# The last expert pair's down weights by halves of the output columns, and the second mixer's first chunk by token blocks, in a model block on one core

## The chip, the cores and the metric

The kernel runs on one core of a Trainium2 chip. The metric is the device time of one execution in microseconds (us), from the first to the last instruction of the core; less is better. TensorE (PE) multiplies, VectorE (DVE), ScalarE (ACT) and GpSimd (POOL) work on elements, SyncE (SP) issues most of the weight loads.

## The reference

256 tokens of width 1024 pass through two blocks. Only this much of the first matters here; the second block (four feed-forward layers and two recurrent mixers) follows it.

```python
for i in range(DEPTH):                       # DEPTH = 2
    mix = even_or_odd_mixer(x, ...)          # i = 1: _mla_gla_mixer, which begins with x @ w_in
    x = _layer_norm(ALPHA * x + mix, ln1_g[i], ln1_b[i])
    ffn = _hier_moe(x, ...)                  # 32 experts, 2 of them for each token
    x = _layer_norm(ALPHA * x + ffn, ln2_g[i], ln2_b[i])

# one expert, with d = 1024 and a hidden width of 512
hdn = jax.nn.silu(xb @ w_gate[e]) * (xb @ w_up[e])
y = hdn @ w_down[e]
```

## The kernel before

Each engine runs a program written out by hand, and semaphores order them against each other. The programs have three parts: part 0 ends in the middle of layer 0's experts, part 1 goes from there to the middle of layer 1's experts, and part 2 does the rest. So the end of an expert stage occurs twice: in part 1 ahead of the second mixer (`od_pe`, `od_act`, `od_dve`), and in part 2 ahead of the first feed-forward layer (`ffn_pe`).

The 32 experts are worked in 16 pairs. The two experts j = 0 and 1 of a pair hold 64 tokens each; the products of expert 0 go to the PSUM partitions 0 to 63, those of expert 1 to 64 to 127, so one product uses 64 of the array's 128 columns (the trace writes 128*64). The weights are float32 and are multiplied as such; the trace records one float32 product as two MATMULs. `paired_pe` (line 1345) takes the products of the two experts in turn. Each pair has 12 loads of 1 MB: gate, up and down, in two halves of the contraction each, for each expert. They go through one queue in the order of use, into a ring of 7 slots and into further places that are lent to it for the stage (`w_parts`, `arena`, `x_high_slot`, `x_low_slot`, `x_tok`).

For pair g PE does gate, up, the combining products of pair g - 1 for token block 0 (`combine_pe`), the transposes of the hidden values, the combining products of block 1, and down into two banks of 512 output columns, n = 0 and 1. The result y is cut into a high and a low part: ACT writes `yh` (line 1438), DVE writes `yl` (line 1468). `combine_pe` multiplies both by the selection matrix (line 228, 128x512), and DVE adds the product to `acc` (`add_dve`, line 1377). `combine_pe` runs for token blocks tb = 0, 1 and for the column halves n = 0, 1 of each.

After the last pair, DVE adds, takes the layer norm's statistics by half rows (`half_stats`, line 665), then mean and variance (672, 674), centres (676), and scales (687) with the reciprocal root that POOL makes. PE transposes the normed tokens (`transpose_x_pe`, line 479), ahead of them go idle products that write nothing of use (`busy_pe`, line 460, 128x512 with the full 128 columns). ACT takes the high part of the transposed tokens (line 495), DVE the low part (504, `x_low_dve`). The weights of the mixers and feed-forward layers are likewise cut in high (432, ACT, `split_act`) and low (439, DVE, `split_dve`) parts, in buffers of half a 1 MB chunk; `ahead` is the first such part of the next stage. `project_pe` multiplies tokens and weights by three products for each pair of parts; a chunk of the second mixer is named `od(i)`, its two parts `od(i) + (0,)` and `od(i) + (1,)`. `project_block_pe` does one token block of a chunk and waits for the low part of its second half.

Of the kernel before, what the change touches and what calls it, by code (L numbers as in the profile page):

```python
# [465 lines left out]

def transpose_x_pe(e, k, n, after=None):
    S = k.S
    for tb in range(NB):
        if n < 0:  # L470
            e.wait_ge(*S.x_loaded[tb][0])
        for half in range(2):
            view = pairs(k.banks.open(e, B_BANKS, ("xT", n, tb, half))[:, :], 4)
            if n >= 0 and half == 0:
                busy_pe(e, k, k.banks["xT", n, tb, half], BUSY[after][tb])
            if n >= 0:
                e.wait_ge(*S.x_tok[n, tb, half])
            for i in range(4):
                ins = e.transpose(view[:, i, :], k.x_tok[:, tb, block(4 * half + i)], k.ident)
            ins.then_inc(*S.turned.tell((n, tb, half)))  # L480
# [187 lines left out]
def norm_centre_dve(e, k, n, tb):  # L668
# [5 lines left out]
    e.tensor_scalar(k.ve[:, tb:tb + 1], k.mv[:, tb, 1:2], LN_EPS, None, ALU.add).then_inc(*S.variance.tell((n, tb)))  # L674
    e.wait_ge(*S.norm_loaded[n])
# [674 lines left out]
def combine_pe(e, k, X, g, tb):  # L1350
# [3 lines left out]
    for n in range(2):  # L1354
# [31 lines left out]
def experts_pe(e, k, X, first, last):  # L1386
    S, b = X.S, k.experts
    gather_pe(e, k, X, first // GATHERED)
    for g in range(first, last):
# [21 lines left out]
        paired_pe(e, k, X, tiles, "down", g, FT_E // 2, b.hT)  # L1411
    for tb in range(NB):
        combine_pe(e, k, X, last - 1, tb)


def experts_act(e, k, X, first, last, ahead=None):
# [3 lines left out]
    for g in range(first, last):  # L1420
# [20 lines left out]
def experts_dve(e, k, X, first, last, ahead=None):  # L1441
# [6 lines left out]
    for g in range(first, last):  # L1448
# [14 lines left out]
        if ahead is not None and g == last - 1:  # L1463
            split_dve(e, k, ahead)
        for n in range(2):
            cols = slice(BANK * n, BANK * n + BANK)
# [1479 lines left out]
```

## Time and profile before

| What | us |
|---|---|
| median of 3 runs | 2320.6 |
| lowest and highest of them | 2320.22, 2322.26 |
| profiled execution, first to last instruction | 2323.1 |
| PE busy | 2166.1 (93%) |
| DVE busy | 1142.2 (49%) |
| ACT busy | 784.0 (34%) |
| end of layer 0's experts to the first projection of the second mixer | 634.70 to 660.38 |
| end of layer 1's experts to the first feed-forward product | 1284.07 to 1308.65 |

The profiled execution has no time of its own beside its span; the span is 2.5 us, or 0.1%, above the median. In a timeline a row gives start, duration, engine, line, operation, what is written from what, shape and count; in brackets stands how long the engine had been idle before it, and who ended that. Several instructions can be merged in one row. Matmul records have about 0.16 us at their end in which the next one already runs.

### The profile page before, as it was taken

To read this page: it belongs to the slowest core of one execution; us is meant where nothing else is said; L and a number is where in the kernel's file an instruction comes from. 1 tells how busy PE (TensorE), PEld (TensorE's weight loads), DVE (VectorE), ACT (ScalarE), POOL (GpSimd) and SP (SyncE) were. 2 spreads that over 40 slices of the span, in tenths; PEclk is the share of its full clock that TensorE was granted. 3 is DMA by queue.
4 is the path that set the end of the run, shared out by engine and by line. 5 is a ranking of instruction groups with operands and counts; after the bars stand their busy time and mean duration, and the time that the engine had idled before them with its cause. 6 is when DMAs were issued, how large, how long until landed. Compare 5 with 4: busy or idle time off the path is not lost.

```text
span 2323.1 us, 30109 instructions
## 1 busy us (share of the span) xinstructions
PE 2166.1 (93%) x12126; PEld 1528.0 (66%) x12126; DVE 1142.2 (49%) x1786; ACT 784.0 (34%) x1299; POOL 61.5 (3%) x62
## 2 busy tenths in 40 slices
PE   8999998899887989997988999999999999989998
PEld 7884443443367944433433688898888788888887
DVE  5582222121156831211111666678666766787666
ACT  3441110111034321101111355454555455554553
POOL 0010000000010100000000000001000000001000
PEclk9999999899998799999999999999999999999999
DMA  9449999999972289999999864634555464534561
GB/s 289 145 175 379 421 421 421 417 421 420 413 246 73 76 363 420 420 421 415 420 420 421 295 209 168 199 128 127 181 200 200 154 208 166 193 96 159 167 208 46
DMA packets 231542, 622.66 MB, mean 268 GB/s; under 512 B 15456, under 2 KB 166944, under 8 KB 182112
## 3 DMA queue, kind: packets, MB, share of 16 engines
q1 hardware_dynamic: 226096, 605.32, 68.7%
q0 software_dynamic: 3040, 10.78, 1.5%
q10 hardware_dynamic: 2256, 4.50, 0.5%
q8 instruction: 102, 1.67, 0.3%
q14 instruction: 48, 0.39, 0.0%
HBM read 619.51 MB, written 1.05 MB: 267 GB/s over the span
## 4 chain that ended last, share of the span: by engine, by line
PE 41%; DMA 6%; DVE 4%; ACT 2%; issue 1%; POOL 0%; SPq 0%; DVEq 0%; ACTq 0%
PE bank L1517 14%; PE bank L1505 10%; PE bank L1518 7%; PE bank L228 6%; PE bank L1345 3%; DMA arena<-in_moe_w_up 1%; DMA ring<-in_moe_w_up 1%; DMA ring<-in_ffn_gate 1%; DMA w_parts<-in_moe_w_up 1%; DMA x_tok<-in_moe_w_up 1%; DVE w_low L439 1%; PE bank L1673 1%; ACT w_high L432 1%; DVE x_tok L687 0%; DVE x_tok L676 0%
## 5 line engine op out<-in xcount | busy, mean ns | idle before, releaser
L439 DVE TENSOR_TENSOR w_low<-ring,w_high 128x1024 fp32r<-128x1024 f32 x364 | 441.1, 1225 | 271.7 <-ACT w_high L432 271.7
L1517 PE MATMUL bank<-xT_parts,w_high 128*128 128x512 f32 x1408 | 496.2, 395 | 6.0 <-DVE xT_parts L504 6.0
L432 ACT ACTIVATE w_high<-ring 128x1024 fp32r<-128x1024 f32 x364 | 377.1, 1053 | 218.0 <-PE bank L1518 184.6
L1518 PE MATMUL bank<-xT_parts,w_low 128*128 128x256 f32 x1408 | 394.5, 280 | 0.0
L1345 PE MATMUL bank<-ring,arena 128*64 128x512 f32 x1344 | 339.0, 594 | 17.3 <-DMA w_parts<-in_moe_w_gate 5.3
L1517 PEld LDWEIGHTS bank<-xT_parts,w_high 128*128 128x128 f32 x1408 | 264.0, 188 | 69.0 <-DVE xT_parts L504 6.9
L1345 PE MATMUL bank<-w_parts,arena 128*64 128x512 f32 x768 | 263.8, 609 | 13.4 <-DMA w_parts<-in_moe_w_up 6.7
L1518 PEld LDWEIGHTS bank<-xT_parts,w_low 128*128 128x128 f32 x1408 | 265.8, 189 | 3.1
L1345 PEld LDWEIGHTS bank<-ring,arena 128*64 128x64 f32 x1344 | 110.1, 137 | 230.5 <-issue 221.9
L1453 DVE SCALAR_TENSOR_TENSOR arena<-arena,bank 128x512 f32<-128x512 f32 x32 | 23.9, 747 | 434.1 <-PE bank L1345 434.1
L228 PE MATMUL bank<-w_high,xT_parts 128*128 128x256 f32 x1152 | 222.9, 290 | 10.4 <-DVE w_low L439 8.8
L228 PEld LDWEIGHTS bank<-w_high,xT_parts 128*128 128x128 f32 x1152 | 186.4, 195 | 13.0 <-ACT arena L564 4.5
L228 PE MATMUL bank<-w_low,xT_parts 128*128 128x256 f32 x576 | 165.0, 286 | 0.0
L1345 PEld LDWEIGHTS bank<-w_parts,arena 128*64 128x64 f32 x768 | 81.1, 140 | 121.3 <-issue 117.0
L1468 DVE TENSOR_TENSOR arena_rounded<-bank,arena_rounded 128x512 fp32r<-128x512 f32 x64 | 41.2, 686 | 217.8 <-ACT arena_rounded L1438 217.8
L1505 PE MATMUL bank<-w_high,hidden_low 128*128 128x512 f32 x320 | 126.3, 395 | 0.0
L1505 PE MATMUL bank<-w_low,hidden_high 128*128 128x512 f32 x320 | 126.2, 394 | 0.0
L1505 PE MATMUL bank<-w_high,hidden_high 128*128 128x512 f32 x320 | 126.1, 394 | 0.0
L228 PE MATMUL bank<-xT_parts,w_high 128*128 128x256 f32 x608 | 115.7, 292 | 9.0 <-DVE xT_parts L504 6.0
L228 PEld LDWEIGHTS bank<-w_low,xT_parts 128*128 128x128 f32 x576 | 112.6, 195 | 0.2
L1438 ACT ACTIVATE arena_rounded<-bank 128x512 fp32r<-128x512 f32 x64 | 34.7, 594 | 229.0 <-PE bank L1345 229.0
L228 PEld LDWEIGHTS bank<-xT_parts,w_high 128*128 128x128 f32 x608 | 98.7, 199 | 10.8 <-issue 5.4
(284 smaller groups left out, 2934.4 us busy)
## 6 DMA issues: line engine op xcount, KB each, us to landing
ring<-in_moe_w_gate SPq DMA_DIRECT2D x56, 1024.0 KB, 24.3
ring<-in_moe_w_up SPq DMA_DIRECT2D x56, 1024.0 KB, 21.0
ring<-in_moe_w_down SPq DMA_DIRECT2D x56, 1024.0 KB, 25.8
ring<-in_ffn_gate SPq DMA_DIRECT2D x44, 1024.0 KB, 6.8
ring<-in_ffn_up SPq DMA_DIRECT2D x44, 1024.0 KB, 5.4
ring<-in_ffn_down SPq DMA_DIRECT2D x44, 1024.0 KB, 6.6
w_parts<-in_moe_w_up SPq DMA_DIRECT2D x32, 1024.0 KB, 26.1
w_parts<-in_moe_w_down SPq DMA_DIRECT2D x32, 1024.0 KB, 26.1
```

The source lines that it names most:

```text
L228: ins = e.matmul(out, lhs, rhs, start=first and i == 0, stop=last and i == len(parts) - 1)
L432: e.activation(hi, src, ACT.Copy).then_inc(*S.high.tell(key))
L439: e.tensor_tensor(lo, src, hi.bitcast(F32), ALU.subtract).then_inc(*S.low.tell(key))
L1345: ins = e.matmul(tile[r, :], lhs[:, half * per + kk, r], X.ring.view(chunks[j])[:, kk, BANK * n:BANK * n + BANK], start=half == 0 and kk = ...
L1438: e.activation(b.yh[:, cols], X.banks[X.key("y", g, n)][:, :], ACT.Copy).then_inc(*S.act_out.tell(X.key("y_high", g, n)))
L1453: e.scalar_tensor_tensor(out=b.silu, in0=b.silu, scalar=b.weight[:, i:i + 1], in1=X.banks[X.key("h", g)][:, :], op0=ALU.mult, op1=ALU.mult ...
L1468: e.tensor_tensor(b.yl[:, cols], X.banks[X.key("y", g, n)][:, :], b.yh[:, cols].bitcast(F32), ALU.subtract).then_inc(*S.dve_out.tell(X.key ...
L1505: ins = e.matmul(out, lhs, rhs[:, 0, cols], start=g == 0 and j == 0, stop=g == FT - 1 and j == 2)
L1517: e.matmul(pairs(bank[:, :]), hi[:, j, :], k.x_parts[:, :, j, :], start=j == 0, stop=False)
L1518: ins = e.matmul(bank[:, 0:T], lo[:, j, :], k.xh[:, j, :], start=False, stop=j == KT - 1)
L1673: ins = e.matmul(scores[:, 2 * i + blk, :], d.decayed[r, j, block(blk)], d.queries(d.decayed[r, j, block(blk)], m), start=True, stop=True)
```

## The change

The four down loads of pair 15 fetch, in place of half of the contraction for all 1024 output columns, the whole contraction for half of the columns (pieces of 512 floats). PE multiplies them with `last_down_pe`: column half 0 for expert 0 and then for expert 1, then the combining products of half 0 for both token blocks, then the same for column half 1. ACT and DVE cut y by column half as each is done. The splitting of `ahead` moves behind that, on DVE behind the second mean. DVE's order of sums, statistics and norm changes with it (`norm_after_experts_dve`), and `norm_centre_dve` is cut in two. In the second mixer, PE transposes token block 0, projects it with `od(0)`, and only then transposes and projects block 1; the idle products ahead of block 1 are gone there. ACT's order of work stays as it is apart from `ahead`.

```diff
+def by_columns(name, g):
+
+    return name == "down" and g == N_PAIRS - 1
+
...
-                    src = rows(w[layer, PAIR * g + j], k)[:, half * per:(half + 1) * per, :]
+                    w_rows = rows(w[layer, PAIR * g + j], k)
+                    src = w_rows[:, :, half * BANK:(half + 1) * BANK] if by_columns(name, g) else w_rows[:, half * per:(half + 1) * per, :]
...
+def last_down_pe(e, k, X, tiles, g, n):
+
+    S, b = X.S, k.experts
+    chunks = [X.key("down", g, n, j) for j in range(PAIR)]
+    for j, chunk in enumerate(chunks):
+        r = slice(CAP * j, CAP * j + CAP)
+        e.wait_ge(*X.ring.landed(chunk))
+        for kk in range(FT_E):
+            ins = e.matmul(tiles[n][r, :], b.hT[:, kk, r], X.ring.view(chunk)[:, kk, :], start=kk == 0, stop=kk == FT_E - 1)
+    ins.then_inc(*S.expert.tell(X.key("down", g, n)))
...
-        paired_pe(e, k, X, tiles, "down", g, FT_E // 2, b.hT)
-    for tb in range(NB):
-        combine_pe(e, k, X, last - 1, tb)
+        if by_columns("down", g):
+            for n in range(2):
+                last_down_pe(e, k, X, tiles, g, n)
+                for tb in range(NB):
+                    combine_pe(e, k, X, g, tb, (n,))
+        else:
+            paired_pe(e, k, X, tiles, "down", g, FT_E // 2, b.hT)
...
-        if ahead is not None and g == last - 1:
-            split_act(e, k, ahead)
-        e.wait_ge(*S.expert[X.key("down", g, 1)])
         for n in range(2):
+            if n == 0 or by_columns("down", g):
+                e.wait_ge(*S.expert[X.key("down", g, n if by_columns("down", g) else 1)])
             cols = slice(BANK * n, BANK * n + BANK)
             e.activation(b.yh[:, cols], X.banks[X.key("y", g, n)][:, :], ACT.Copy).then_inc(*S.act_out.tell(X.key("y_high", g, n)))
...
-    project_pe(e, k, od(0), fresh=n)
+    bank = k.banks.open(e, A_BANKS, od(0))
+    for tb in range(NB):
+        transpose_block_pe(e, k, n, tb, 0 if tb else BUSY["experts"][0])
+        project_block_pe(e, k, od(0), bank, tb, n)
...
-def norm_after_experts_dve(e, k, X, n):
-
+def norm_after_experts_dve(e, k, X, n, ahead):
+
+    g = N_PAIRS - 1
+    y_low_dve(e, k, X, g, 0)
     added_stats_dve(e, k, X, n, 0, 0)
+    added_stats_dve(e, k, X, n, 1, 0)
+    y_low_dve(e, k, X, g, 1)
     added_stats_dve(e, k, X, n, 0, 1)
+    norm_mean_dve(e, k, n, 0)
     norm_centre_dve(e, k, n, 0)
-    added_stats_dve(e, k, X, n, 1, 0)
+    added_stats_dve(e, k, X, n, 1, 1)
     norm_scale_dve(e, k, n, 0)
-    added_stats_dve(e, k, X, n, 1, 1)
+    norm_mean_dve(e, k, n, 1)
+    split_dve(e, k, ahead)
+    x_low_dve(e, k, n, 0, 0)
+    x_low_dve(e, k, n, 0, 1)
     norm_centre_dve(e, k, n, 1)
-    x_low_dve(e, k, n, 0, 0)
     norm_scale_dve(e, k, n, 1)
```

In the order of instructions a matmul counts once for each product, where the trace has two records for a float32 one.

On PE, the second half of the last pair's down products in layer 0 (chunks in `x_low_slot` and `x_tok`), with what follows, stood so before:

```order
L1345 MATMUL bank<-x_low_slot,arena 64x512
L1345 MATMUL bank<-x_tok,arena 64x512
L1345 MATMUL bank<-x_low_slot,arena 64x512
L1345 MATMUL bank<-x_tok,arena 64x512
L228 MATMUL bank<-arena_rounded 128x512 x8
L460 MATMUL bank<-tables 128x512 x4
L479 MATMUL bank<-tables,x_tok 128x128 x8
L460 MATMUL bank<-tables 128x512 x4
L479 MATMUL bank<-tables,x_tok 128x128 x8
```

In the changed kernel all down products of the last pair, with what follows, stand so:

```order
L1374 MATMUL bank<-w_parts,arena 64x512 x4
L1374 MATMUL bank<-x_high_slot,arena 64x512 x4
L228 MATMUL bank<-arena_rounded 128x512 x4
L1374 MATMUL bank<-x_low_slot,arena 64x512 x4
L1374 MATMUL bank<-x_tok,arena 64x512 x4
L228 MATMUL bank<-arena_rounded 128x512 x4
L466 MATMUL bank<-tables 128x512 x4
L484 MATMUL bank<-tables,x_tok 128x128 x8
L228 MATMUL bank<-w_high_53,xT_parts 128x256
```

The products of the two experts no longer take turns: four of one stand ahead of four of the other. The combining products of column half 0 stand ahead of the products of column half 1, and the first projection stands behind the transposes of block 0.

On PE, the second token block of the second mixer's chunk `od(0)` begins so in the changed kernel (`w_high_54` belongs to its second part, and block 0 ends with the first two rows):

```order
L228 MATMUL bank<-w_low_58,xT_parts 128x256
L228 MATMUL bank<-w_high_54,xT_parts 128x256
L484 MATMUL bank<-tables,x_tok 128x128 x8
L228 MATMUL bank<-w_high_53,xT_parts 128x256
L228 MATMUL bank<-w_low_57,xT_parts 128x256
```

The eight transposes of block 1 moved from ahead of the projection to its middle.

On DVE, the end of the norm ahead of the second mixer stood so before, from the last sum on (`w_low_58` is the second part of `od(0)`, `w_low_55` the first of `od(1)`):

```order
L1377 TENSOR_TENSOR acc<-acc,bank 128x512
L665 BN_STATS bn<-acc 128x6
L672 BN_AGGR mv<-bn 128x2
L674 TENSOR_SCALAR var_eps<-mv 128x1
L676 SCALAR_TENSOR_TENSOR x_tok<-acc,mv,norm_gb 128x1024
L504 TENSOR_TENSOR xT_parts<-bank,xT_parts 128x4x128
L687 SCALAR_TENSOR_TENSOR x_tok<-x_tok,rstd,norm_gb 128x512 x2
L504 TENSOR_TENSOR xT_parts<-bank,xT_parts 128x4x128 x3
L439 TENSOR_TENSOR w_low_58<-ring,w_high_54 128x1024
L439 TENSOR_TENSOR w_low_55<-ring,w_high_51 128x1024
```

In the changed kernel it stands so, from the last sum on:

```order
L1405 TENSOR_TENSOR acc<-acc,bank 128x512
L675 BN_STATS bn<-acc 128x6
L703 SCALAR_TENSOR_TENSOR x_tok<-x_tok,rstd,norm_gb 128x512 x2
L682 BN_AGGR mv<-bn 128x2
L684 TENSOR_SCALAR var_eps<-mv 128x1
L445 TENSOR_TENSOR w_low_57<-ring,w_high_53 128x1024
L514 TENSOR_TENSOR xT_parts<-bank,xT_parts 128x4x128 x2
L692 SCALAR_TENSOR_TENSOR x_tok<-acc,mv,norm_gb 128x1024
L703 SCALAR_TENSOR_TENSOR x_tok<-x_tok,rstd,norm_gb 128x512 x2
L445 TENSOR_TENSOR w_low_58<-ring,w_high_54 128x1024
L514 TENSOR_TENSOR xT_parts<-bank,xT_parts 128x4x128 x2
L445 TENSOR_TENSOR w_low_55<-ring,w_high_51 128x1024
```

The splitting of `ahead` (`w_low_57`) and both low parts of block 0 moved between the last mean and the centring of block 1; the splitting of `w_low_58` moved ahead of the low parts of block 1.

## Rows read from the trace of the kernel before

**Rows 1.** The page: the span and the engines' busy times.

```profile
span 2323.1 us, 30109 instructions
PE 2166.1 (93%) x12126; PEld 1528.0 (66%) x12126; DVE 1142.2 (49%) x1786; ACT 784.0 (34%) x1299; POOL 61.5 (3%) x62
```

**Rows 2.** Timeline of PE, end of layer 1's experts.

```profile
1277.81 3.65 PE L1345 MATMUL bank<-arena 128*64 128x512 f32 x16 [1.32 <-DMA arena<-in_moe_w_up]
...
1282.96 1.17 PE L228 MATMUL bank<-arena_rounded 128*128 128x512 f32 x4
1284.07 0.64 PE L1345 MATMUL bank<-w_parts,arena 128*64 128x512 f32 x1
1284.08 0.64 PE L1345 MATMUL bank<-x_high_slot,arena 128*64 128x512 f32 x1
...
1293.77 2.23 PE L228 MATMUL bank<-arena_rounded 128*128 128x512 f32 x8 [2.26 <-DVE arena_rounded L1468]
1295.84 3.60 PE L460 MATMUL bank<-tables 128*128 128x512 f32 x8
...
1308.65 0.47 PE L1517 MATMUL bank<-xT_parts,w_high 128*128 128x512 f32 x1 [1.50 <-DVE xT_parts L504]
```

**Rows 3.** Groups on PE by shape, 686 to 690.5 us: products with 96 and 64 columns.

```profile
L228 PE MATMUL bank<-arena,wide_tables 128*96 128x256 f32 x8 | 1.9, 385 | 0.5 <-DVE arena L2117 0.5
L228 PE MATMUL bank<-arena,wide_tables 128*64 128x256 f32 x4 | 1.1, 392 | 0.0
```

**Rows 4.** Timeline of ACT, end of layer 1's experts.

```profile
1290.64 1.06 ACT L432 ACTIVATE w_high<-ring 128x1024 fp32r<-128x1024 f32 x1 [6.80 <-DMA ring<-in_ffn_gate]
1291.60 1.07 ACT L1438 ACTIVATE arena_rounded<-bank 128x512 fp32r<-128x512 f32 x2
```

**Rows 5.** Timeline of DVE, end of layer 1's experts.

```profile
1292.94 1.28 DVE L1468 TENSOR_TENSOR arena_rounded<-bank,arena_rounded 128x512 fp32r<-128x512 f32 x2
1294.51 0.69 DVE L1377 TENSOR_TENSOR acc<-acc,bank 128x512 f32<-128x512 f32 x1 [0.28 <-PE bank L228]
...
1297.59 1.27 DVE L676 SCALAR_TENSOR_TENSOR x_tok<-acc,mv,norm_gb 128x1024 f32<-128x1024 f32 x1
1298.78 0.68 DVE L1377 TENSOR_TENSOR acc<-acc,bank 128x512 f32<-128x512 f32 x1
...
1300.10 1.40 DVE L687 SCALAR_TENSOR_TENSOR x_tok<-x_tok,rstd,norm_gb 128x512 f32<-128x512 f32 x2
...
1304.97 1.41 DVE L687 SCALAR_TENSOR_TENSOR x_tok<-x_tok,rstd,norm_gb 128x512 f32<-128x512 f32 x2
1306.29 2.22 DVE L504 TENSOR_TENSOR xT_parts<-bank,xT_parts 128x512 fp32r<-128x512 f32 x3
```

**Rows 6.** Timelines of PE, DVE and ACT, layer 0's last pair to chunk `od(1)`.

```profile
634.70 0.64 PE L1345 MATMUL bank<-w_parts,arena 128*64 128x512 f32 x1
...
645.16 0.69 DVE L1377 TENSOR_TENSOR acc<-acc,bank 128x512 f32<-128x512 f32 x1 [0.29 <-PE bank L228]
...
656.41 1.38 PE L479 MATMUL bank<-tables,x_tok 128*128 128x128 f32 x8
...
659.07 1.22 DVE L439 TENSOR_TENSOR w_low<-ring,w_high 128x1024 fp32r<-128x1024 f32 x1
...
660.38 0.35 PE L228 MATMUL bank<-w_high,xT_parts 128*128 128x256 f32 x1 [2.59 <-DVE w_low L439]
...
660.67 2.00 ACT L432 ACTIVATE w_high<-ring 128x1024 fp32r<-128x1024 f32 x2 [2.24 <-issue]
...
661.76 2.36 DVE L439 TENSOR_TENSOR w_low<-ring,w_high 128x1024 fp32r<-128x1024 f32 x2 [1.48 <-ACT w_high L432]
...
667.90 0.38 ACT L749 ACTIVATE acc<-bank 128x256 f32<-128x256 f32 x1 [5.22 <-PE bank L228]
```

**Rows 7.** Busy time, granted clock and DMA in stretches of the second mixer.

```profile
662.00:664.00 2.00, 2.00 (x11) 2.00 (x11) 2.00 (x2) 0.68 (x1) 0.00 (x0) 0.50 1.02 350
666.00:668.00 2.00, 2.00 (x19) 2.00 (x18) 0.00 (x0) 0.10 (x1) 0.00 (x0) 1.00 0.97 380
...
690.00:700.00 10.00, 10.00 (x63) 7.36 (x63) 5.57 (x9) 3.50 (x5) 0.00 (x0) 1.00 0.00 0
760.00:770.00 10.00, 10.00 (x82) 10.00 (x81) 9.72 (x21) 2.87 (x6) 0.00 (x0) 0.50 0.00 0
```

The columns are the stretch and its length, busy us and count of PE, PEld, DVE, ACT and POOL, the granted clock of PE as a share of 2.4 GHz, the busy share of the DMA engines, and GB/s.

More of the change, by code:

```diff
@@ L464, with transpose_block_pe @@
 BUSY = {"mixer": (0, 4), "experts": (4, 4), "ffn": (0, 4)}
+def transpose_block_pe(e, k, n, tb, busy=0):
+    S = k.S
+    if n < 0:
+        e.wait_ge(*S.x_loaded[tb][0])
+    for half in range(2):
+        view = pairs(k.banks.open(e, B_BANKS, ("xT", n, tb, half))[:, :], 4)
+        if half == 0:
+            busy_pe(e, k, k.banks["xT", n, tb, half], busy)
+        if n >= 0:
+            e.wait_ge(*S.x_tok[n, tb, half])
+        for i in range(4):
+            ins = e.transpose(view[:, i, :], k.x_tok[:, tb, block(4 * half + i)], k.ident)
+        ins.then_inc(*S.turned.tell((n, tb, half)))
 def transpose_x_pe(e, k, n, after=None):
-    S = k.S
     for tb in range(NB):
[L470 to L480, printed above, removed]
+        transpose_block_pe(e, k, n, tb, BUSY[after][tb] if n >= 0 else 0)
 def x_parts_at(k, n, tb, half):
@@ L674, in norm_centre_dve @@
     e.tensor_scalar(k.ve[:, tb:tb + 1], k.mv[:, tb, 1:2], LN_EPS, None, ALU.add).then_inc(*S.variance.tell((n, tb)))
+def norm_centre_dve(e, k, n, tb):
+    S = k.S
+    e.wait_ge(*S.norm_step[n, tb, "mean"])
     e.wait_ge(*S.norm_loaded[n])
@@ L1347, in paired_pe, with combine_pe @@
         ins.then_inc(*X.S.expert.tell(X.key(name, g, half)))
-def combine_pe(e, k, X, g, tb):
+def last_down_pe(e, k, X, tiles, g, n):
[7 more added lines that the diff above has]
+    ins.then_inc(*S.expert.tell(X.key("down", g, n)))
+def combine_pe(e, k, X, g, tb, columns=(0, 1)):
     S, b = X.S, k.experts
     turned = b.selT[:, g % (2 * GATHERED), block(tb)]
-    for n in range(2):
+    for n in columns:
         cols = slice(BANK * n, BANK * n + BANK)
@@ L1432, in experts_act, with y_low_dve, experts_dve @@
             e.wait_ge(*S.product[X.key("combine", g - 1, 1, 1)])
-        if ahead is not None and g == last - 1:
-            split_act(e, k, ahead)
-        e.wait_ge(*S.expert[X.key("down", g, 1)])
         for n in range(2):
+            if n == 0 or by_columns("down", g):
+                e.wait_ge(*S.expert[X.key("down", g, n if by_columns("down", g) else 1)])
             cols = slice(BANK * n, BANK * n + BANK)
             e.activation(b.yh[:, cols], X.banks[X.key("y", g, n)][:, :], ACT.Copy).then_inc(*S.act_out.tell(X.key("y_high", g, n)))
-def experts_dve(e, k, X, first, last, ahead=None):
+    if ahead is not None:
+        split_act(e, k, ahead)
+def y_low_dve(e, k, X, g, n):
+    S, b, cols = X.S, k.experts, slice(BANK * n, BANK * n + BANK)
+    e.wait_ge(*S.act_out[X.key("y_high", g, n)])
+    e.tensor_tensor(b.yl[:, cols], X.banks[X.key("y", g, n)][:, :], b.yh[:, cols].bitcast(F32), ALU.subtract
+                    ).then_inc(*S.dve_out.tell(X.key("y", g, n)))
+def experts_dve(e, k, X, first, last, norm_follows=False):
     S, b = X.S, k.experts
@@ L1462, in experts_dve @@
             e.wait_ge(*S.product[X.key("combine", g - 1, 1, 1)])
-        if ahead is not None and g == last - 1:
-            split_dve(e, k, ahead)
+        if norm_follows and g == last - 1:
+            return
         for n in range(2):
-            cols = slice(BANK * n, BANK * n + BANK)
-            e.wait_ge(*S.act_out[X.key("y_high", g, n)])
-            e.tensor_tensor(b.yl[:, cols], X.banks[X.key("y", g, n)][:, :], b.yh[:, cols].bitcast(F32), ALU.subtract
-                            ).then_inc(*S.dve_out.tell(X.key("y", g, n)))
-    if ahead is None:
-        combine_dve(e, k, X, last - 1)
+            y_low_dve(e, k, X, g, n)
+    combine_dve(e, k, X, last - 1)
 def experts_sp(e, k, X):
@@ L1956, in od_pe @@
     cos, sin, swap = (k.tab(name)[ROPES, :] for name in ("mla_cos", "mla_sin", "mla_swap"))
-    project_pe(e, k, od(0), fresh=n)
+    bank = k.banks.open(e, A_BANKS, od(0))
+    for tb in range(NB):
+        transpose_block_pe(e, k, n, tb, 0 if tb else BUSY["experts"][0])
+        project_block_pe(e, k, od(0), bank, tb, n)
     project_pe(e, k, od(1))
@@ L2649, in pe_program @@
         experts_pe(e, k, k.main[0], CUT, N_PAIRS)
-        transpose_x_pe(e, k, 1, "experts")
         od_pe(e, k, 1)
```

22 lines of the change are left out of this document (15 added, 7 removed).

## Prediction, made before the changed kernel ran

> **What bounds the kernel now.** I read the page first: PE is busy for 93% of the span [rows 1], so what counts is where PE waits, and whether the work behind such a place starts late with it. The timelines of PE, ACT and DVE show two such places, the ends of the two expert stages. Up to there the loads set the pace: the last up chunk ends a wait for a DMA at 1277.81 [rows 2]. Behind it, 16 records of down in `w_parts` and `x_high_slot` start at 1284.07, and PE does not wait for a chunk again. From there a chain of PE, ACT and DVE sets the time: down, yh, yl, combining, sum, statistics, norm, transposes, low parts, first product. From the start of down (s) to DVE's first sum (A) it takes 1294.51 - 1284.07 = 10.44 us in layer 1 [rows 2, 5] and 645.16 - 634.70 = 10.46 us in layer 0 [rows 6]. From A to the first feed-forward product it takes 1308.65 - 1294.51 = 14.14 us [rows 2, 5].
>
> What starts late behind these places stays late. In the second mixer PE is busy for 10.00 of 10 us [rows 7], the later experts follow from its result, and the feed-forward layers keep PE busy to the end (93% over all [rows 1]). So I count each us at these two places in full.
>
> **The loads.** By columns, a row of a chunk is fetched in 2 KB pieces. The trace has 1 KB pieces at 350 GB/s when the engines are busy [rows 7]; before that the up chunks came 2 MB in about 5 us, 420 GB/s. If 2 KB pieces were as slow as 1 KB ones, each MB would take 3.0 in place of 2.5 us and the fourth chunk would land 2 us later; if they are as fast as now, 0. The last up chunk lands at 1277.8 and four chunks at 2.5 us make 1287.8 for the last, 1289.8 at worst. PE starts on the first at 1284.07, 3.8 us after its landing (3.3 at worst), and by what follows on the last some 16 us later. So either end costs nothing. Without that cover it would be up to 2 us for each layer.
>
> **The down products.** This is the term on which all rests. Now a product of expert 0 and one of expert 1 start 0.01 us apart (1284.07, 1284.08) and run beside each other in the two column halves of the array [rows 2]. 16 records in 8 such pairs take 3.65 us from first start to last end, like the 16 of the up chunk at 1277.81 [rows 2]. A single stream of float32 records of 512 elements takes 3.60 us for 8, 0.43 us each (the idle products, 128 columns wide) [rows 2]. A stream with only 64 columns is not faster: 4 records of 256 elements, 1.1 us busy, against 8 in 1.9 us with 96 columns [rows 3], which is about 0.25 us each, half a 512 element record. So a pair costs what one of its members costs, and taking turns is worth a factor of 2. The new order gives it up: four products (8 records) of expert 0, then four of expert 1, in order. A chunk takes 8 x 0.43 = 3.44 us, a column half 6.88, with 0.16 us at the end 7.0. Down takes 13.8 us of PE in each layer, where two halves of 3.5 were enough.
>
> The Trainium skill (TensorE: Matmul & The Clock Gate, Part 3, "What overlaps and what doesn't") says that matmuls start and end strictly in program order. By that page different tile positions may run together, so the last record of expert 0 and the first of expert 1 would overlap; that is 0.4 us for each of two handovers in each layer, and the sum would be 1.7 us lower.
>
> **From s to A after the change.** Column half 0: 7.0 us. Then ACT yh 0.6 (1.07 for two [rows 4], plus latency), 0.1 to DVE, yl 0.69, 0.14 to PE (1292.94 + 0.69 to 1293.77 [rows 2, 5]), with 0.03 ahead of ACT 1.56 us. PE stands in all of that, since the combining products of half 0 are ahead of the chunks of half 1 in its queue, and these chunks have long landed. The four combining records take 1.10 us until the next product may start (1282.96 to 1284.07 [rows 2]). Column half 1: 7.0 us, then 1.56 us for its yh and yl, and 0.74 us from the combining product to the sum (1293.77 to 1294.51 [rows 2, 5]). Together 7.0 + 1.56 + 1.10 + 7.0 + 1.56 + 0.74 = 18.96 us, against 10.44. A comes 8.5 us later. What was gained, the sums and statistics of half 0 for both blocks, lies beside the second 7.0 us.
>
> **From A to the first feed-forward product, layer 1.** DVE from A: sum, statistics, mean and variance of block 0, 3.08 - 1.33 = 1.75 (A to centring is 3.08, 1294.51 to 1297.59, with one sum and statistics more than now; such a pair is 1298.78 to 1300.10, 1.32 to 1.33); centring 1.19 (1297.59 to 1298.78); sum and statistics 1.32; scaling 1.32 (1304.97 to 1306.29); mean and variance 0.43; then the moved splitting of `ahead` 1.18; two low parts 1.48; centring 1.19 [rows 5, 6]. The splitting lay in the wait for down before and cost nothing; now it is on the path. That puts the start of the second scaling at A + 9.86. From there to the first product it is 3.68 us now (1304.97 to 1308.65 [rows 2, 5]) and 3.8 then, as the last low part now waits for ACT. 13.66 against 14.14: 0.5 us gained. Layer 1: 8.5 - 0.5 = **+8.0 us**.
>
> **The second mixer's chunk by blocks, layer 0.** Second scaling at A + 9.86, 1.32 long, then the low part of `od(0)`'s second half, from whose start it is 1.31 us to the product (659.07 to 660.38 [rows 6]): PE begins block 0 at A + 12.5. Before, it began at A + 15.2, so here the blocks do give 2.7 us. But the transposes of block 1 now stand behind 24 products. At full clock these take 0.12 us each, 2.9 us; at half clock 0.21, 5.1 (19 and 11 in PE count for 2 us, rounded [rows 7]). PE will have been idle for about 6 us, and now it drops to 0.50 after 2.6 us of waiting [rows 6, 7], so that the 48 products of `od(0)` take 7.4 us (660.38 to 667.8) in place of 5.8, 1.6 us lost; with that I take 4.5. So block 1 is transposed at A + 17.0 and no longer at 656.41, A + 11.25. ACT waits for it: the queue is in order, and the high parts of block 1, five DMA issues and then the splitting of `od(1)` stand behind. The latter starts 4.26 us after the transposes begin (656.41 to 660.67), and DVE has the low parts 3.45 us after that (661.76 + 2.36 [rows 6]). `od(1)` can start at A + 24.8. Block 1 of `od(0)` is done earlier, A + 17.0 + 3.0 + 2.9 = 22.9, and PE waits 1.9 us. Before, `od(1)` followed without a wait at about 667.8, A + 22.6. So the blocks lose 2.2 us: 0.6 if PE keeps its clock, 2.8 if it stays at half. Layer 0: 8.5 + 2.2 = **+10.7 us**.
>
> **Sum.** 8.0 + 10.7 = 18.7 us. The profiled execution would have a span of 2341.8 and the median run 2320.6 + 18.7 = **2339.3 us**, 0.8% more. A change under 0.2%, 4.6 us, could not be told from none.
>
> **Rivals.** (1) *The experts' products overlap all the same.* If the array runs the four products of expert 1 beside those of expert 0 though they are issued later, or if a lone 64 column stream goes at twice the pace, a chunk costs 1.75 us. Then s to A is 3.65 + 1.56 + 1.10 + 3.65 + 1.56 + 0.74 = 12.3 us, A moves by 1.8, layer 1 costs 1.3 and layer 0 between 2.4 and 4.6, together 3.7 to 5.9 us; with the clock kept it is 2324.3, not slower by the bound. It decides if a chunk takes under some 1.85 us. For it speaks only that the two streams share rows of the array; [rows 3] and the idle products [rows 2] speak against. 10%.
> (2) *The clock.* With 6 us idle ahead of `od(0)` and new gaps around it, PE may lie at half clock through `od(0)` and into `od(1)`, whose 48 products then cost up to 4 us more, or the stretch at 0.50 around 760 [rows 7] may be longer by its new start: 2343 to 2346. For it: the drop after 2.6 us now. Against: PE gets full work from `od(1)` on. 12%.
> (3) *The stretch at half clock is shorter.* At 760 to 770 PE and DVE are both busy (10.00 and 9.72 [rows 7]), so little of it would come back; I allow 8 us: 2331. 6%.
> (4) *It does what its shape suggests*: half 0 is wholly hidden and half 1 ends earlier. This asks that PE had waited for the last chunks, so that the work for half 0 filled a wait; PE starts them 3.8 us late. It would save half of yh, yl and combining and one sum, about 3.5 us a layer: 2313.6. 5%.
>
> **Chances.** My forecast 67% (own range 2334 to 2343), the rivals as given. Faster 0.05; same 0.07, most of rival 1; slower 0.88. The range from 2326 to 2345 leaves out rival 4, most of rival 1 and the top of rival 2.
>
> **What would show it.** In the profile after, 8 records each from `w_parts`, `x_high_slot`, `x_low_slot` and `x_tok` in this order, 3.4 us a chunk and one stream at a time; a PE wait of about 1.6 us for yl between the second and third; DVE's sum of block 0, half 1, some 19 us after the first down record; PE waiting about 6 us ahead of `od(0)`, then about 2 us for DVE's low part of `od(1)`. I am wrong if records of the two experts start together, if the chunks land after PE asks for them, or if the mixer and the experts behind it catch up with a late start.

## The result and the profile after

The changed kernel takes 2338.66 us (median of 4 runs, 2337.18 to 2339.01) against 2321.43 us for the kernel before on the same chip (4 runs, 2320.22 to 2323.11). The medians are 17.2 us apart; the ratio on record is 1.0064, with an interval of 1.0051 to 1.0076, that is 12 to 18 us slower. The forecast was 2339.3 us and slower. Its direction and its two places hold, and so do most of its waits. But the largest term of its sum was too big, since the two experts' products overlapped in part where it let them run one after the other, and a term behind the two places was missing. That 2338.66 lies within 1 us of 2339.3 is luck: measured again, the same kernel came to 2336.78 us against 2323.58 (experiment 10).

The page of the changed kernel begins so, to be read against [rows 1]:

```profile
span 2335.4 us, 30115 instructions
PE 2169.8 (93%) x12118; PEld 1530.2 (66%) x12118; DVE 1144.3 (49%) x1786; ACT 783.5 (34%) x1299; POOL 62.2 (3%) x62
```

The busy times have hardly moved; what was added is waiting, and matmuls that no longer run beside each other. The two spans differ by 12.3 us only, as this execution reached the last pair of layer 0 1.8 us earlier (632.94 against 634.70 [rows 6]), before anything that was changed. So the places are compared from the first down record of the last pair, called s.

The timeline of PE in the changed kernel, end of layer 1's experts (s = 1289.51), answers to [rows 2]:

```profile
1289.51 2.33 PE L1374 MATMUL bank<-w_parts,arena 128*64 128x512 f32 x5
1291.25 0.64 PE L1374 MATMUL bank<-x_high_slot,arena 128*64 128x512 f32 x1
1291.68 0.59 PE L1374 MATMUL bank<-w_parts,arena 128*64 128x512 f32 x1
1291.73 0.59 PE L1374 MATMUL bank<-x_high_slot,arena 128*64 128x512 f32 x1
...
1292.59 2.31 PE L1374 MATMUL bank<-x_high_slot,arena 128*64 128x512 f32 x5
1296.54 1.15 PE L228 MATMUL bank<-arena_rounded 128*128 128x512 f32 x4 [1.64 <-DVE arena_rounded L1481]
1297.62 2.36 PE L1374 MATMUL bank<-x_low_slot,arena 128*64 128x512 f32 x5
...
1304.54 1.16 PE L228 MATMUL bank<-arena_rounded 128*128 128x512 f32 x4 [1.50 <-DVE arena_rounded L1481]
...
1318.54 0.77 PE L1557 MATMUL bank<-xT_parts,w_high 128*128 128x512 f32 x1 [1.50 <-DVE xT_parts L514]
```

Expert 0 (`w_parts`) starts alone. Beside its fifth record the first of expert 1 (`x_high_slot`) starts at 1291.25, and from there both run beside each other until expert 0 is through: four records of the two overlap, 12 pitches of 0.43 us in place of 8 in turns or 16 one after the other. A column half takes 1292.59 + 2.31 - 1289.51 = 5.39 us. Behind it PE waits 1.64 us for yl of half 0, with the chunks of half 1 behind that wait in its queue. They have landed by then: in experiment 5 the last of the four ends a wait at s + 4.45.

DVE in the same stretch answers to [rows 5]:

```profile
1305.28 0.69 DVE L1405 TENSOR_TENSOR acc<-acc,bank 128x512 f32<-128x512 f32 x1 [0.88 <-PE bank L228]
...
1311.20 1.22 DVE L445 TENSOR_TENSOR w_low<-ring,w_high 128x1024 fp32r<-128x1024 f32 x1
1312.33 1.28 DVE L514 TENSOR_TENSOR xT_parts<-bank,xT_parts 128x512 fp32r<-128x512 f32 x2
1313.53 1.28 DVE L692 SCALAR_TENSOR_TENSOR x_tok<-acc,mv,norm_gb 128x1024 f32<-128x1024 f32 x1
```

The sum of block 0, half 1, comes at s + 15.77, where DVE's first sum was at s + 10.44. The moved splitting and the low parts of block 0 lie on the path, as forecast. In layer 0 (s = 632.94) PE's rows around the token blocks, to be read against [rows 6], are:

```profile
660.89 0.58 PE L228 MATMUL bank<-w_high,xT_parts 128*128 128x256 f32 x1 [5.70 <-DVE w_low L445]
...
666.18 1.23 PE L484 MATMUL bank<-tables,x_tok 128*128 128x128 f32 x8
669.07 0.36 PE L228 MATMUL bank<-w_high,xT_parts 128*128 128x256 f32 x1 [1.67 <-DVE xT_parts L514]
...
673.49 0.35 PE L228 MATMUL bank<-w_high,xT_parts 128*128 128x256 f32 x1 [1.31 <-DVE w_low L445]
```

There are three waits where there was one: 5.70 us ahead of block 0, 1.67 between transposes and projection of block 1, 1.31 ahead of `od(1)`. And block 0 takes 666.18 - 660.89 = 5.3 us. The stretch of it in the view of windows, read as in [rows 7], shows why:

```profile
662.00:664.00 2.00, 2.00 (x11) 2.00 (x11) 0.00 (x0) 0.00 (x0) 0.00 (x0) 0.50 0.90 326
```

The granted clock is 0.50: 11 records are counted in 2 us, where [rows 7] has 19 at 1.00.

### The profile page after: what moved, and what is told of

Read it like the earlier page. It is cut to its first block, busy times and chain, and to the rows that moved or that the text cites. A ratio compares the mean times of both kernels' runs of the same rounds, so it can differ in the third digit from the quotient of the medians.

```text
span 2335.4 us, 30115 instructions
## 1 busy us (share of the span) xinstructions
PE 2169.8 (93%) x12118; PEld 1530.2 (66%) x12118; DVE 1144.3 (49%) x1786; ACT 783.5 (34%) x1299; POOL 62.2 (3%) x62
## 3 DMA queue, kind: packets, MB, share of 16 engines
q8 instruction: 102, 1.67, 0.3%
## 4 chain that ended last, share of the span: by engine, by line
PE 41%; DMA 6%; DVE 4%; ACT 2%; issue 1%; POOL 0%; DVEq 0%; SPq 0%; ACTq 0%
PE bank L1557 14%; PE bank L1545 10%; PE bank L1558 7%; PE bank L228 6%; PE bank L1361 3%; DMA arena<-in_moe_w_up 2%; DMA ring<-in_moe_w_up 1%; DMA w_parts<-in_moe_w_up 1%; DMA x_tok<-in_moe_w_up 1%; DVE w_low L445 1%; PE bank L1713 1%; ACT w_high L438 1%; DVE x_tok L703 0%; PE bank L1374 0%; DVE x_tok L692 0%
## 5 line engine op out<-in xcount | busy, mean ns | idle before, releaser
L1361 PE MATMUL bank<-ring,arena 128*64 128x512 f32 x1344 | 339.0, 594 | 17.2 <-DMA w_parts<-in_moe_w_gate 5.3
L1361 PE MATMUL bank<-w_parts,arena 128*64 128x512 f32 x752 | 254.7, 604 | 13.2 <-DMA w_parts<-in_moe_w_up 6.5
L228 PE MATMUL bank<-w_high,xT_parts 128*128 128x256 f32 x1152 | 226.2, 293 | 16.4 <-DVE w_low L445 13.2
```

Source lines behind the costliest of these rows:

```text
L228: ins = e.matmul(out, lhs, rhs, start=first and i == 0, stop=last and i == len(parts) - 1)
L1361: ins = e.matmul(tile[r, :], lhs[:, half * per + kk, r], X.ring.view(chunks[j])[:, kk, BANK * n:BANK * n + BANK], start=half == 0 and kk = ...
```

## Experiments

All are read at the same marks, in us from s, each in one profiled execution. "Mean" is DVE's first mean and variance, "od(1)" ACT's first look at the projected second chunk (squares), "layer 1" the first feed-forward product. The ratio is to the kernel before on the same chip. Its interval reaches 2 to 3 us to either side, so two ratios that lie 2 or 3 us apart don't tell which kernel is the faster; there the marks have to.

| Kernel | end of down | mean | od(1) | layer 1 | ratio (interval) |
|---|---|---|---|---|---|
| before | 7.4 | 13.2 | 39.0 | 24.6 | 1 |
| changed | 13.5 | 17.2 | 46.6 | 29.0 | 1.0064 (1.0051 to 1.0076) |
| 1 turns | 10.0 | 13.7 | 43.2 | 25.6 | 1.0029 (1.0019 to 1.0040) |
| 2 no blocks | 13.5 | 17.2 | 40.2 | 29.0 | 1.0032 (1.0019 to 1.0044) |
| 3 blocks alone | 7.4 | 13.2 | 42.7 | 24.6 | 1.0021 (1.0012 to 1.0029) |
| 4 half 0 between | 16.1 | 19.8 | 42.3 | 31.1 | 1.0036 (1.0023 to 1.0050) |
| 5 the same, split late | 9.4 | 13.2 | 35.7 | 24.5 | 0.9982 (0.9973 to 0.9991) |
| 6 next chunk first | 13.5 | 17.2 | 44.8 | 29.0 | 1.0046 (1.0031 to 1.0062) |
| 7 sixteen in a row | 13.9 | 19.0 | 45.7 | 30.4 | 1.0076 (1.0060 to 1.0091) |
| 8 idle products | 13.5 | 17.2 | 44.2 | 29.0 | 1.0032 (1.0020 to 1.0044) |
| 9 groups of two | 10.1 | 13.8 | 43.1 | 25.6 | 1.0028 (1.0019 to 1.0038) |
| 10 changed again | 13.5 | 17.2 | 46.4 | 29.0 | 1.0060 (1.0046 to 1.0073) |

Down and mean are those of layer 1; layer 0 has the same within 0.15 us, but for experiment 7 (down at 14.9, mean at 19.9).

**1. The products take turns again.** The two chunks of a half are waited for together.

```diff
-    for j, chunk in enumerate(chunks):
-        r = slice(CAP * j, CAP * j + CAP)
-        e.wait_ge(*X.ring.landed(chunk))
-        for kk in range(FT_E):
+    for chunk in chunks:
+        e.wait_ge(*X.ring.landed(chunk))
+    for kk in range(FT_E):
+        for j, chunk in enumerate(chunks):
+            r = slice(CAP * j, CAP * j + CAP)
             ins = e.matmul(tiles[n][r, :], b.hT[:, kk, r], ...)
```

> The changed kernel, but within each column half the products of the two experts take turns again, as in the kernel before. Theory A (the lost pairing is the main cost): the changed kernel's trace shows 12 record pitches of 0.43 us for a column half, 5.2 us, since four records of the second expert run beside the last four of the first; in turns it is 8 pitches, 3.65 us with the end. From the first down record to DVE's sum of block 0, half 1, 15.8 us become 12.5, in each layer, and the whole is 6.5 us faster than the changed kernel. Rival B (a product's time hangs on the way the loads are cut, not on the order of the products): a column half stays at 5.2 to 5.4 us and the time at that of the changed kernel.

Measured: down ends 3.5 us earlier in each layer, and od(1) and layer 1 come 3.4 us earlier; the ratio falls from 1.0064 to 1.0029, some 8 us. PE starts in pairs again:

```profile
1286.68 0.64 PE L1375 MATMUL bank<-w_parts,arena 128*64 128x512 f32 x1
1286.68 0.64 PE L1375 MATMUL bank<-x_high_slot,arena 128*64 128x512 f32 x1
1287.16 0.59 PE L1375 MATMUL bank<-w_parts,arena 128*64 128x512 f32 x1
1287.16 0.59 PE L1375 MATMUL bank<-x_high_slot,arena 128*64 128x512 f32 x1
...
1291.97 1.17 PE L228 MATMUL bank<-arena_rounded 128*128 128x512 f32 x4 [1.64 <-DVE arena_rounded L1482]
```

Theory A holds, rival B falls. The lost turns are about half of the change's cost. Against the kernel before, 1.0 us is left at the first feed-forward product and 4.2 at od(1). A part of it is seen in the last row: PE still waits 1.64 us for yl of half 0.

**2. The changed kernel without token blocks.**

```diff
-    bank = k.banks.open(e, A_BANKS, od(0))
-    for tb in range(NB):
-        transpose_block_pe(e, k, n, tb, 0 if tb else BUSY["experts"][0])
-        project_block_pe(e, k, od(0), bank, tb, n)
+    transpose_x_pe(e, k, n, "experts")
+    project_pe(e, k, od(0), fresh=n)
```

> The changed kernel, but the second mixer's chunk is projected as before: both token blocks are transposed (with the idle products ahead of block 1), then both projected. Theory A (block 1's transposes behind block 0's projection hold up ACT, and through it the next chunk): from DVE's sum of block 0, half 1, to the first product of the next chunk 24.8 us become about 22.1 (the part after that sum is 0.5 to 0.9 us shorter in layer 1 as well), so 2 to 3 us less in all. Rival B (the blocks gain what they seem to, an early start of the projection): it becomes 1 to 2 us slower than the changed kernel.

Measured: od(1) at 40.2 in place of 46.6, 6.4 us earlier, more than twice the 2 to 3 us expected; rival B has the wrong sign. PE's timeline, and DVE's row of the weights' low part, say where it comes from:

```profile
655.54 3.60 PE L466 MATMUL bank<-tables 128*128 128x512 f32 x8
659.60 1.38 PE L484 MATMUL bank<-tables,x_tok 128*128 128x128 f32 x8 [0.46 <-DVE x_tok L703]
661.44 0.36 PE L228 MATMUL bank<-w_high,xT_parts 128*128 128x256 f32 x1 [0.46 <-issue]
...
660.12 1.22 DVE L445 TENSOR_TENSOR w_low<-ring,w_high 128x1024 fp32r<-128x1024 f32 x1
```

The first projection starts at s + 28.0 (s = 633.44), where it starts in the changed kernel too (28.0). In both it starts as the low part of the weights is done: here that is at 660.12 + 1.22 = 661.34, 0.10 us ahead of PE, though the bracket names no releaser. Without blocks, the idle products and the transposes of block 1 lie in that time and cost nothing; with blocks the transposes come later, the idle products are gone, and the clock falls. So the blocks had no start to gain.

**3. Token blocks alone, on the kernel before.**

```diff
-    project_pe(e, k, od(0), fresh=n)
+    bank = k.banks.open(e, A_BANKS, od(0))
+    for tb in range(NB):
+        transpose_block_pe(e, k, n, tb, 0 if tb else BUSY["experts"][0])
+        project_block_pe(e, k, od(0), bank, tb, n)
...
-        x_low_rest_dve(e, k, 1)
+        x_low_dve(e, k, 1, 0, 1)
         split_dve(e, k, od(0) + (1,))
+        x_low_dve(e, k, 1, 1, 0)
+        x_low_dve(e, k, 1, 1, 1)
```

> The kernel before, with the projection by token blocks alone: block 0 transposed and projected, then block 1, without idle products ahead of block 1; on DVE the second weight part of that chunk is split ahead of block 1's low parts. Down weights, their order and the rest of the norm stay as before. Theory A: the next chunk starts 2 to 3 us later from DVE's first sum than the 22.6 us before, and the time is 2 to 3 us above the kernel before, with nothing else changed in either expert stage. Rival B: it starts no later, and all of the change's cost is in the down products.

Measured: down, mean and layer 1 are those of the kernel before, od(1) is 3.8 us later, the ratio 1.0021. Theory A holds in kind, but the cost is above the 2 to 3 us that it gave. The earlier split of `od(0)`'s second part on DVE belongs to this edit: block 0 starts at s + 24.1, some 1.5 us ahead of the projection before (25.7), and od(1) is late all the same.

**4. Half 0's combining products within half 1's down products.**

```diff
+            last_down_pe(e, k, X, tiles, g, 0)
+            last_down_pe(e, k, X, tiles, g, 1, range(FT_E // 2))
+            for tb in range(NB):
+                combine_pe(e, k, X, g, tb, (0,))
+            last_down_pe(e, k, X, tiles, g, 1, range(FT_E // 2, FT_E))
+            for tb in range(NB):
+                combine_pe(e, k, X, g, tb, (1,))
```

The products take turns, the projection is not by blocks, and `split_act` and `split_dve` of `ahead` stand ahead of yh and yl of half 0.

> Built from what the trace shows: loads by columns stay; the products take turns; the combining products of half 0 stand in the middle of half 1's down products, where their yl is ready, so that PE doesn't wait for it; the splitting of the next stage's first part stands ahead of y again, in the wait; the projection is not by blocks. Theory A: 3.65 + 3.65 us down with 1.1 between, then 1.56 + 0.74 to the sum of block 0, half 1, at 10.7 us after the first down record, and 12.1 us from there to the first feed-forward product (13.3 less the 1.2 of the moved split): 22.8 us against 24.6 in the kernel before and 29.0 in the changed one. Two layers: 3 to 4 us faster than the kernel before. Rival B (norm and sums on DVE are the bound either way): within 1 us of the kernel before. ACT's wait for the first weights of the next stage shows what the 2 KB pieces cost: it ended 6.6 us after the first down record before; up to 2 us more if they are as slow as 1 KB pieces.

Measured: neither theory; down ends at s + 16.1 and the kernel is slower than the one before. ACT's and PE's rows (s = 1289.79) show a wait that I had not reckoned with:

```profile
1297.10 1.06 ACT L438 ACTIVATE w_high<-ring 128x1024 fp32r<-128x1024 f32 x1 [7.53 <-DMA ring<-in_ffn_gate]
1298.06 0.58 ACT L1479 ACTIVATE arena_rounded<-bank 128x512 fp32r<-128x512 f32 x1
```

```profile
1300.23 2.05 PE L228 MATMUL bank<-arena_rounded 128*128 128x512 f32 x4 [4.09 <-DVE arena_rounded L1486]
1302.20 1.12 PE L1375 MATMUL bank<-x_low_slot,arena 128*64 128x512 f32 x1
```

The first weights of the next stage land at s + 7.3. In the kernel before this wait was over at s + 6.6, ahead of y's end at 7.4, and cost next to nothing. With y in halves, yh of half 0 could start at s + 3.7, and the same wait ahead of it holds up ACT, DVE and PE. PE waits 4.09 us, then works at half clock (granted clock 0.50 from 1300 to 1304, 1.12 us for this record in place of 0.64).

**5. The same with the split between the halves of y.**

```diff
             e.activation(b.yh[:, cols], X.banks[X.key("y", g, n)][:, :], ACT.Copy).then_inc(...)
+            if ahead is not None and g == last - 1 and n == 0:
+                split_act(e, k, ahead)
...
     y_low_dve(e, k, X, g, 1)
+    split_dve(e, k, ahead)
     added_stats_dve(e, k, X, n, 0, 1)
```

> The fourth experiment again, with the splitting of the next stage's first part moved: ACT does it between yh of half 0 and yh of half 1, DVE behind yl of half 1. Theory A (in the fourth experiment ACT's wait for the next stage's weights, which land 7.3 us after the first down record, stood ahead of yh of half 0 and held up PE for 4.1 us): the first down record to DVE's sum of block 0, half 1, falls from 18.3 to about 11.7 us, to the first feed-forward product from 31.1 to about 24, against 24.6 in the kernel before and 29.0 in the changed one. The time is then within 0.1% of the kernel before or up to 2 us faster. Rival B (the combining products between the down products break the pairing or the wait for the fourth chunk at 4.3 us is the bound): the sum stays above 14 us.

Measured: theory A holds. Layer 1 is at 24.5 and od(1) at 35.7, 3.3 us ahead of the kernel before; the ratio is 0.9982, some 4 us, the only kernel here that is faster than the one before. That is more than the 2 us that theory A allowed. PE's rows (s = 1284.06):

```profile
1288.51 0.61 PE L1375 MATMUL bank<-x_low_slot,arena 128*64 128x512 f32 x1 [0.80 <-DMA x_tok<-in_moe_w_down]
...
1290.38 1.20 PE L228 MATMUL bank<-arena_rounded 128*128 128x512 f32 x4
...
1294.96 1.17 PE L228 MATMUL bank<-arena_rounded 128*128 128x512 f32 x4 [1.52 <-DVE arena_rounded L1486]
```

The combining products of half 0 no longer wait. The fourth chunk ends a wait at s + 4.45. The last up chunk lands with s as before, and at 2.5 us a chunk the fourth would be there at s + 3.7: the 2 KB pieces cost 0.7 us over 4 MB, an estimate from these rows. Experiment 4 gives as much: ACT's wait for the next stage's weights ended 12.83 us behind the start of the last up chunk's products before (1290.64 - 1277.81), and 13.58 us there (1297.10 - 1283.52). In layer 1 the gain ahead of the second scaling is used up by DVE, which scales block 1 at s + 20.9 here as in the kernel before. In layer 0 the first projection starts at s + 23.6 against 25.7, as the weights' low part stands ahead of block 1's. That is 2.1 of the 3.3 us; the rest comes behind that start, where the clock did not fall. No run parted the two.

**6. The second chunk is split ahead of block 1's parts**, on ACT and DVE, in the changed kernel.

```diff
-        split_x_act(e, k, 1)
+        split_block_act(e, k, 1, 0)
+        split_chunk(e, k, od(1), split_act)
+        split_block_act(e, k, 1, 1)
```

> The changed kernel, but ACT and DVE split the mixer's second chunk ahead of block 1's high and low parts, and so ahead of the DMA issues. Theory A (in the changed kernel PE's 1.3 us ahead of that chunk is ACT's queue, stuck behind block 1's transposes): the 1.3 us wait goes, the rest stays, in all 1.3 us less in layer 0 and nothing in layer 1. The 5 us from the serial order itself (transposes and parts of block 1 between the two blocks, 3 us idle, and half clock) stay. Rival B: the order of ACT costs nothing, and PE waits for something else there.

Measured: od(1) 1.8 us earlier, 1.6 against experiment 10, layer 1 unchanged, and no wait ahead of `od(1)` is left on PE. DVE makes the low parts of the second half of `od(0)` and of both halves of `od(1)` in one go, while PE is at block 0 (663.38 to 668.60):

```profile
662.11 3.49 DVE L445 TENSOR_TENSOR w_low<-ring,w_high 128x1024 fp32r<-128x1024 f32 x3
```

Theory A holds: that wait was ACT's queue, and DVE's behind it.

**7. Sixteen records in a row**, on the kernel before: in the last pair expert 0's products for both halves of the contraction and both banks stand ahead of expert 1's.

```diff
+            for half in range(2):
+                for j in range(PAIR):
+                    e.wait_ge(*X.ring.landed(X.key("down", g, half, j)))
+            for j in range(PAIR):
+                r = slice(CAP * j, CAP * j + CAP)
+                for half in range(2):
+                    for kk in range(2):
+                        for n, tile in enumerate(tiles):
...
```

> The kernel before, but in the last pair all 16 down records of expert 0 stand ahead of all 16 of expert 1 (loads, y, combining and the mixer as before; PE first waits for all four chunks, which at most costs what they land later than 3.7 us after the first record would have started). It tells how the two streams overlap when they don't take turns. Theory A (the second stream starts when four of the first one's records are left, as the trace of the changed kernel shows for 8 and 8): 28 pitches of 0.43 us, 12.0 us and 0.2 at the end. Rival B (half of the shorter stream always overlaps): 24 pitches, 10.5 us. Rival C (my prediction's rule, no overlap): 32 pitches, 13.9 us. The kernel before has 16 pitches, 7.4 us.

PE's rows, layer 1 (expert 0 in `w_parts` and `x_low_slot`, expert 1 in `x_high_slot` and `x_tok`):

```profile
1294.01 5.31 PE L1420 MATMUL bank<-w_parts,arena 128*64 128x512 f32 x8 [3.72 <-DMA x_tok<-in_moe_w_down]
1299.16 2.31 PE L1420 MATMUL bank<-x_low_slot,arena 128*64 128x512 f32 x5
1300.88 0.64 PE L1420 MATMUL bank<-x_high_slot,arena 128*64 128x512 f32 x1
...
1304.36 3.60 PE L1420 MATMUL bank<-x_tok,arena 128*64 128x512 f32 x8
```

Expert 1 starts behind 13 of expert 0's 16 records, beside the thirteenth: again four overlap. Down takes 1307.96 - 1294.01 = 13.9 us, which is what rival C gives, but by another way: the first eight records took 5.31 us in place of 3.60, at half clock after the wait of 3.72 us. Without these 1.7 us it is 12.2, theory A's number; layer 0 comes to 12.2 as well (14.9 less 6.25 - 3.60). The starts, which the clock doesn't touch, decide between A and C.

**8. Idle products in the wait ahead of block 0**, in the changed kernel.

```diff
         transpose_block_pe(e, k, n, tb, 0 if tb else BUSY["experts"][0])
+        if tb == 0:
+            busy_pe(e, k, bank, 6)
```

> The changed kernel with six idle products (12 records, 5.2 us) in PE's 5.7 us of waiting between the transposes and the projection of block 0. Theory A (the 24 products of block 0 take 5.3 us and not 2.9 since the clock fell to half in that wait): the clock stays at 1.00, block 0 takes 2.9 us, the next chunk starts 2 to 2.4 us earlier. Rival B (the clock falls all the same, or the products wait for something else): no change, or up to 0.5 us more if the idle products run past the wait.

The windows view of this kernel, in block 0's projection (start 661.69, end 664.67):

```profile
662.00:664.00 2.00, 2.00 (x19) 2.00 (x18) 0.00 (x0) 0.00 (x0) 0.00 (x0) 1.00 0.65 262
```

Block 0 takes 3.0 us in place of 5.3, od(1) comes 2.4 us earlier. Theory A holds. The ratio falls by more, some 7 us. Of that the profiled executions show 4.1 us from s of layer 0 to the end: the 2.4, and 1.7 behind the first feed-forward product, where the clock held in this one (see below). The rest is not accounted for; it is no more than the two intervals leave open.

**9. Turns by two products**, in the changed kernel.

```diff
+    for k0 in range(0, FT_E, 2):
+        for j, chunk in enumerate(chunks):
+            r = slice(CAP * j, CAP * j + CAP)
+            for kk in (k0, k0 + 1):
...
```

> The changed kernel, but within a column half the experts take turns by two products (four records) in place of four products (eight records). PE waits for both chunks ahead of each half, as with full turns. Theory A (a record of one expert may start past up to three waiting ones of the other, so runs of four pair up wholly and a run of eight leaves four alone): a column half takes 3.65 us as with turns by one product, and the first down record to the end of down is 10.0 us as in the first experiment. Rival B (half of each run overlaps, whatever its length): a column half takes 10 pitches, 4.5 us, and down ends at about 11.8 us.

PE's first rows (s = 1286.59):

```profile
1286.59 0.64 PE L1376 MATMUL bank<-w_parts,arena 128*64 128x512 f32 x1
1286.61 0.64 PE L1376 MATMUL bank<-x_high_slot,arena 128*64 128x512 f32 x1
```

Though four records of expert 0 stand first in the program, expert 1's first one starts 0.02 us after the first of them. Down ends at 10.1: theory A; rival B is out.

**10. The changed kernel again.**

> The changed kernel once more, on the same chip as the ninth experiment, to see how much of its profile repeats. Theory A: first down record to the end of down 13.5 us, to the first feed-forward product 29.0, to the squares of the mixer's second chunk 46.6, each within 0.2 us; only s and where the clock falls ahead of and behind these places differ. Rival B: the pairing of the last four records is a chance of that one execution, and the end of down moves by a us or more.

Measured: down, mean and layer 1 agree within 0.02 us, od(1) within 0.22; the ratio is 1.0060. Theory A.

## Why the prediction came out as it did

**What bounds the kernel; the loads.** Right. A late start at these places stayed late: of od(1)'s delay of 7.6 us all 7.6 were left at the routing of the second expert stage (DVE writes `gate_w` at 838.3 and 832.5; 838.3 - 632.94 against 832.5 - 634.70), and s of layer 1 follows that by 451.2 us, against 451.6. That also settles rival 3: the stretch at 0.50 lies in between, 755 to 790 now and 750 to 785 before, and gave nothing back. The loads cost nothing in the changed kernel, since they are covered; experiment 5 takes part of the cover away and finds 0.7 us, within the bounds of 0 and 2. (The last chunk is first used at s + 9.9; I wrote some 16 us, where my own terms give 13. Nothing hung on it.)

**The down products.** That the lost turns cost time, and where, was right; how much was not. The step that failed is "so a pair costs what one of its members costs ... a column half 6.88, with 0.16 us at the end 7.0": I let the two streams run strictly one after the other. Measured is 5.39 us, as the last four records of one run beside the first four of the other. Between my 7.0 and the 3.65 of rival 1 that is about half way, and my own sign of being wrong, records of the two experts that start together, is in the trace at 1291.25. With 5.4 in place of 7.0 twice, and 1.64 and 1.50 us for the two waits, s to the sum is 15.8 and not 18.96, and the delay 5.3 and not 8.5 us in each layer: 6.4 us too much in the sum. The Trainium skill (TensorE: Matmul & The Clock Gate, Part 3, "What overlaps and what doesn't") has matmuls start and end strictly in program order; here they do not, by the starts 1291.25 and 1291.68 above and by those of experiments 7 and 9, and the measurement decides. The 0.4 us that I worked out by that page for a handover is 1.7, four pitches of 0.43.

**From the sum to the first feed-forward product.** Forecast 13.66, measured 1318.54 - 1305.28 = 13.26 (14.14 before). Layer 1 lost 4.4 us by the marks, where 8.0 were forecast.

**The token blocks.** Forecast from the sum to `od(1)` 24.8 us, measured 673.49 - 648.73 = 24.76, 2.2 more than before, as forecast. So good a fit is partly luck, as three errors cancel: block 0 starts at 12.16 (12.5), takes 5.3 (4.5), all at half clock, and from block 1's transposes to `od(1)` it is 7.3 us (7.8). The 0.12 and 0.21 us for a product are not what 19 and 11 in 2 us give (0.11 and 0.18), but they are right: 24 products take 3.0 us at full clock (experiment 8) and 5.3 at half. Rival 2 happened in part: the clock was at half through block 0, and full from block 1 on. But I wrote that "here the blocks do give 2.7 us" for the earlier start, and that is wrong: experiment 2 starts as early without them. It was DVE's order that gave it, and the blocks' own cost within the changed kernel is 6.4 us, where my terms give 2.2 + 2.7 = 4.9. Undone one at a time, the clock is 2.4 of it (experiment 8) and ACT's queue 1.6 to 1.8 (6). The rest, a difference that no run isolates, is left for the transposes and parts of block 1 between the two projections. On the kernel before the blocks cost 3.8 (3).

**What was missing.** At the first feed-forward products the granted clock fell in the changed kernel, in both of its profiled executions, which it did not in the one of the kernel before (its row stands second):

```profile
1318.00:1320.00 2.00, 1.46 (x5) 1.30 (x6) 2.00 (x3) 1.56 (x2) 0.00 (x0) 0.63 0.86 264
1320.00:1322.00 2.00, 2.00 (x8) 1.71 (x8) 2.00 (x3) 0.00 (x0) 0.00 (x0) 0.52 0.99 283
```

```profile
1308.00:1310.00 2.00, 1.35 (x8) 1.22 (x8) 2.00 (x3) 1.68 (x2) 0.00 (x0) 1.00 0.96 199
```

A pair of records takes 0.64 us there and 0.35 later. It costs 1.6 us: ACT's next split, which waits for these products, starts 4.68 us behind the first of them (1323.22 - 1318.54), and 3.12 us in experiment 8, at full clock.

It does not always follow from the change: experiments 6 and 8 have the same marks up to there and full clock. In all, it fell in four of the seven profiled executions with the changed kernel's order of the norm (changed, 10, 1 and 2; not 6, 8 and 9), and in none of the five others. That points to the order of the norm but doesn't show it.

From the first feed-forward product to the end it is 1016.9 us against 1014.5, 2.4 us. Only the 1.6 are explained, and even the 2.4 can't be charged to the change with safety: over all twelve profiles this stretch is between 1012.3 and 1016.9 us, and in experiment 2, where the clock fell too, 1013.8.

**The sum.** By marks: 7.6 us (layer 0, to the second routing), - 0.4 (to s of layer 1), 4.4 (layer 1) and 2.4 (from there on) are 14.0 us, where the ratio gives 14.9 (11.8 to 17.6). The forecast had 18.7: 6.4 too much for down, 2.4 too little for what lies behind layer 1, and some tenths elsewhere. The time fell into the stated range and into my own of 2334 to 2343; that the median also nearly met the forecast is owed to these errors and to the spread of the runs, not to the sum. Rival 4 did not happen, as PE had waited for no chunk; but its aim can be reached, by another order (experiment 5).

## What to carry to other kernels

When an order of products is changed for the sake of what comes behind it, look first at which products run beside each other now: two streams in different column halves of the array cost as much as one, but only while they stand close together in the program. Work in halves pays only if the engine that feeds the next step isn't made to wait between them: put what depends on half 0 where its operands are ready, and check for each wait that is moved or passed when it ends, not only how long it was. A step that seems to start something earlier may only stand beside the edit that does; undo them one at a time. And compare a forecast with the result term by term, since a total can fit while its terms do not.

## What the runs showed of the hardware

In these runs PE starts a matmul record ahead of earlier ones that wait for their column half, if it needs the other half. A run of four records of one expert in front of four of the other loses nothing (10.1 us down against 10.0 with turns by single products, experiments 9 and 1). Runs of eight and of sixteen leave all but the last four alone, so the start of the second stream came beside record 5 of 8 and 13 of 16. It looks as if a record may pass three waiting ones; that this is a fixed number of places, and whether weight loads count among them, no run tells.
